# Value products of head pairs on the two halves of the output's rows, with the queries as columns, in block two's attentions

## What is computed

```
ya = spatial_gating(...)
yb = chunk_band_attention(heads(bq), heads(bk), heads(bv), b_rel)
yc = dsa_attention(heads(cq), heads(ck), heads(cv), iq, ik, iw, t5_table)
ym = memory_attention(heads(mq), km, vm)
mixed = concatenate([ya * silu(a_g), yb * silu(bg), yc * silu(cg), ym * silu(mg)])
y = mixed @ w_out + b_out
```

## Time and profile before

| | |
|---|---|
| Time, three runs | 3182.13 us median, 3174.91 to 3184.65 |
| The profiled execution: its own time and its span | 3182.28 us, span 3180.4 us |
| PE busy over the span | 3014.5 us (95%) |
| DVE, ACT, POOL busy | 1965.4, 1187.2, 490.2 us |
| The three attentions of block two | 1746 to 1948 us of the span |

### The profile page before, as it was taken

How to read it: one execution, slowest core, us unless ns; L and a number is a source line. 1 busy time by engine, 2 the same in 40 slices (tenths; PEclk the granted TensorE clock), 3 DMA queues, 4 the chain that set the end, 5 groups by cost and what they waited for, 6 DMA issues and landing times. The chain is left out here.

```text
span 3180.4 us, 38641 instructions
## 1 busy us (share of the span) xinstructions
PE 3014.5 (95%) x14576; PEld 2429.5 (76%) x14576; DVE 1965.4 (62%) x3282; ACT 1187.2 (37%) x2227; POOL 490.2 (15%) x465
## 2 busy tenths in 40 slices
PE   7999999999899999989999979999889999999999
PEld 6787876777788888777787878645668788888887
DVE  6111744699899946838988336799875444444444
ACT  2221331477677842224475554102561111111110
POOL 1000002355111100221244142010010000000000
PEclk9999999999899999999999989999899999999999
DMA  7323124543844334341255262311101111111111
GB/s 248 139 80 108 52 77 160 189 131 126 223 107 107 113 147 173 117 120 27 81 181 190 83 202 86 123 59 48 34 34 44 67 53 40 51 43 53 53 40 67
DMA packets 190771, 324.08 MB, mean 102 GB/s; under 512 B 16434, under 2 KB 113874, under 8 KB 190586
## 3 DMA queue, kind: packets, MB, share of 16 engines
q1 hardware_dynamic: 169722, 248.72, 25.4%
q0 software_dynamic: 20864, 72.89, 6.3%
HBM read 232.14 MB, written 88.11 MB: 101 GB/s over the span
## 5 line engine op out<-in xcount | busy, mean ns | idle before, releaser
L216 PE MATMUL banks<-b3mlpw_part,b3mlp_acthi 128*128 128x512 f32 x1024 | 315.4, 389 | 0.0
L216 PE MATMUL banks<-b3h4a_hi,b3mlpw_part 128*128 128x512 f32 x960 | 298.2, 389 | 2.1 <-DVE b3mlpw_part L3949 2.1
L428 PE MATMUL banks<-b1ln_w,b_hThi 128*128 128x512 f32 x768 | 239.8, 394 | 3.3 <-DVE b_hTlo L335 3.3
L3994 DVE TENSOR_TENSOR b3out_x<-b3out_x,banks 128x1024 f32<-128x1024 f32 x128 | 154.7, 1218 | 111.7 <-PE banks L216 111.7
L216 PEld LDWEIGHTS banks<-b3mlpw_part,b3mlp_acthi 128*128 128x128 f32 x1024 | 192.3, 188 | 39.9
L3965 ACT ACTIVATE b3mlp_relu<-banks 128x1024 f32<-128x1024 f32 x32 | 32.9, 1027 | 493.0 <-PE banks L216 493.0
L216 PEld LDWEIGHTS banks<-b3h4a_hi,b3mlpw_part 128*128 128x128 f32 x960 | 180.0, 188 | 43.2 <-DVE b3mlpw_part L3949 2.6
L530 PE MATMUL banks<-b_hThi,b1item_hi 128*128 128x512 f32 x464 | 196.4, 423 | 3.4 <-DVE b1item_lo L519 3.1
L216 PE MATMUL banks<-b3mlpw_part,b3mlp_actlo 128*128 128x512 f32 x512 | 199.4, 389 | 0.0
L216 PE MATMUL banks<-b3out_lo,b3mlpw_part 128*128 128x512 f32 x480 | 189.8, 395 | 0.0
L3983 DVE TENSOR_TENSOR b3mlp_relu<-b3mlp_relu 128x1024 f32<-128x1024 f32 x32 | 39.2, 1224 | 239.1 <-ACT b3mlp_relu L3965 239.1
(11 more groups left out here) (501 smaller groups left out, 6934.8 us busy)
## 6 DMA issues: line engine op xcount, KB each, us to landing
qk_spill<-b1scan_qk SPq DMA_DIRECT2D x64, 256.0 KB, 2.9
b1att_k<-qk_spill SPq DMA_DIRECT2D x64, 256.0 KB, 7.5
b1out_ws<-in_w_out SPq DMA_DIRECT2D x16, 1024.0 KB, 4.9
b3mlpw_stage<-in_w_mlp_down SPq DMA_DIRECT2D x16, 1024.0 KB, 4.9
b2h_stage<-in_w_in SPq DMA_DIRECT2D x30, 512.0 KB, 5.2
b3mlpw_stage<-in_w_mlp_up SPq DMA_DIRECT2D x15, 1024.0 KB, 5.1
b1item_stage<-in_w_in SPq DMA_DIRECT2D x29, 512.0 KB, 4.3
b1ln_stage<-in_w_in SPq DMA_DIRECT2D x12, 1024.0 KB, 5.2
```

The costliest lines, as they stand in the source:

```text
L216: last = pe.matmul(out, x, y, start=i == 0, stop=i == n - 1)
L428: last = pe.matmul(K.bank[n % 6], a, b, start=part + k + c == 0, stop=part + k + c == 6)
L3994: v.tensor_tensor(K.m4.x3[:, st], K.m4.x3[:, st], pair, ALU.add).then_inc(S["ml_acc"], 1)
```

## The change

The value products change sides. Before, `turned` (keys x queries) was the stationary operand and the values (keys x 64) the moving one, so that the queries were rows. Now a head's values (64 columns) are stationary and `turned` (128 queries) moves: the output is 64 rows x 128 queries, and heads h and h+1 go to rows 0 to 63 and 64 to 127 of the same columns, their products taking turns. Both heads of a pair are done in one round, r = u+5 for even u. The output is already in the layout of the gate, so the multiplication into `C.rows` and the two transposes are gone. Instead TensorE spreads 1/sum over rows with four products of a broadcast column and the unit matrix. VectorE multiplies the gate with them (in place), then the value products with that. The results of band and memory overwrite their own gates, and the stores read them there; the sparse ones go to `C.outT` as before. SyncE now waits for the stores before it loads over the gates.

```diff
@@ attention_rest, saved, sp_attend
     pass_stored(K, sp, A.kind + "g")
+    if A.sel:
+        saved(K, sp, K.m_band)
     for i in range(2):
         L.start(sp, (A.kind, "g", i), A.gate[:, i], K.pass_dram[A.kind + "g"][i, 0])
+def saved(K, e, A):
+    for i in range(2):
+        e.wait_ge(*K.stores[("b2y", A.k0 + i)])
     attended(K, sp, K.m_mem)
+    saved(K, sp, K.m_mem)
@@ pe_attend
-        u = r - 4
-        if 0 <= u < ALL_UNITS:
+        u = r - 5
+        if 0 <= u < ALL_UNITS and u % 2 == 0:
...
-            pe.wait_ge(S["at_copied"], u + 1)
-            out = K.bank[4 + T % 2][:, h * HD:(h + 1) * HD]
-            products(pe, out, [(C.turned[u % 3][:, i], val) for i, val in enumerate(A.vals(h, t))]).then_inc(S["at_av"], 1)
-        u = r - 6
-        if u >= 0 and u % 4 == 3:
-            T = u // 4
-            pe.wait_ge(S["at_norm"], T + 1)
-            for i in range(2):
-                last = pe.transpose(K.bank[4 + T % 2][:, 256 + i * P:256 + (i + 1) * P], C.rows[T % 2][:, i * P:(i + 1) * P], K.eye)
-            last.then_inc(S["at_flip"], 1)
+            pe.wait_ge(S["at_copied"], u + 2)
+            out = K.bank[4 + T % 2][:, h // 2 * P:(h // 2 + 1) * P]
+            vals = [A.vals(h + g, t) for g in range(2)]
+            for i in range(len(vals[0])):
+                for g in range(2):
+                    last[g] = pe.matmul(out[g * HD:(g + 1) * HD], vals[g][i], C.turned[(u + g) % 3][:, i], start=i == 0, stop=i == len(vals[0]) - 1)
+            for g in range(2):
+                last[g].then_inc(S["at_av"], 1)
+            if h == 2:
+                pe.wait_ge(S["at_one"], T + 1)
+                for i in range(4):
+                    spread = pe.matmul(K.bank[4 + T % 2][i % 2 * HD:(i % 2 + 1) * HD, 256 + i // 2 * P:256 + (i // 2 + 1) * P],
+                                       row_ones(K, T)[:, i:i + 1].to_broadcast([P, HD]), K.eye, start=True, stop=True)
+                    if i >= 2:
+                        spread.then_inc(S["at_flip"], 1)
@@ act_attend
-                a.wait_ge(S["at_av"], u - 2)
+                a.wait_ge(S["at_av"], (u - 3) // 2 * 2 + 2)
@@ dve_attend
-        u = r - 5
-        if 0 <= u < ALL_UNITS and u % 4 == 3:
...
-            v.tensor_tensor(C.rows[T % 2]..., K.bank[4 + T % 2][:, 0:256]..., over(row_ones(K, T), 2, HD), ALU.mult).then_inc(S["at_norm"], 1)
-        u = r - 7
+        u = r - 6
         if u >= 0 and u % 4 == 3:
...
-                if A.u0:
-                    for i in range(2):
-                        v.wait_ge(*K.stores[("b2y", A.last_k0 + i)])
...
+            v.wait_ge(S["at_flip"], 2 * T + 2)
+            gate, bank = A.gate[:, :, cols], K.bank[4 + T % 2].rearrange("p (a s) -> p a s", s=P)
+            v.tensor_tensor(gate, gate, bank[:, 2:4], ALU.mult).then_inc(S["at_norm"], 1)
+            v.wait_ge(S["at_av"], u + 1)
+            v.wait_ge(S["at_norm"], T + 1)
+            v.tensor_tensor(A.out[:, :, cols], bank[:, 0:2], gate, ALU.mult).then_inc(S["at_gate"], 1)
@@ memory map
+    band.out, mem.out, dsa.out = band.gate, mem.gate, C.outT
```

More of the change, by code:

```diff
@@ L3004, in pe_attend @@
             transposed(pe, bank_span(K, bank, width), [C.maps[u % 4][:, i * P:(i + 1) * P] for i in range(width // P)], K.eye).then_inc(S["at_turned"], 1)
-        u = r - 4
-        if 0 <= u < ALL_UNITS:
+        u = r - 5
+        if 0 <= u < ALL_UNITS and u % 2 == 0:
             A, h, t = stage_of(K, u)
-            T = u // 4
+            T, last = u // 4, [None, None]
             if u % A_UNITS == 0:
@@ L3093, in dve_attend @@
                 v.tensor_tensor_reduce(e, bank, bias, -1.0, 3e38, ALU.add, ALU.min, s[:, 0:1]).then_inc(S["at_shift"], 1)
-        u = r - 5
-        if 0 <= u < ALL_UNITS and u % 4 == 3:
[L3096 to L3101, removed]
-        u = r - 7
+        u = r - 6
         if u >= 0 and u % 4 == 3:
             A, h, t = stage_of(K, u)
+            T, cols = u // 4, slice(t * P, (t + 1) * P)
             if t == 0:
@@ L3107, in dve_attend @@
                     v.wait_ge(*K.loads[(A.kind, "g", i)])
-                if A.u0:
-                    for i in range(2):
-                        v.wait_ge(*K.stores[("b2y", A.last_k0 + i)])
-            cols = slice(t * P, (t + 1) * P)
-            v.wait_ge(S["at_flip"], u // 4 + 1)
-            v.tensor_tensor(C.outT[:, :, cols], K.bank[4 + u // 4 % 2][:, 256:512].rearrange("p (a s) -> p a s", a=2), A.gate[:, :, cols], ALU.mult).then_inc(S["at_gate"], 1)
+            v.wait_ge(S["at_flip"], 2 * T + 2)
[4 more added lines that the diff above has]
+            v.tensor_tensor(A.out[:, :, cols], bank[:, 0:2], gate, ALU.mult).then_inc(S["at_gate"], 1)
         if r == ALL_UNITS:
@@ L3147, in pool_attend @@
             for i in range(2):
-                K.stores.start(g, ("b2y", A.k0 + i), K.yT2_dram[A.k0 + i], C.outT[:, i])
+                K.stores.start(g, ("b2y", A.k0 + i), K.yT2_dram[A.k0 + i], A.out[:, i])
 def attend_over(K, e):
@@ L4132, in block_two_memory, with stage @@
     m.bs, m.g, m.b = a.take("bs", [P, 2, P]), a.take("g", [P, GW]), a.take("b", [P, GW])
-    def stage(kind, order, k0, last):
+    def stage(kind, order, k0):
         A = Part()
-        A.kind, A.u0, A.k0, A.last_k0, A.sel = kind, order * A_UNITS, k0, last, {}
+        A.kind, A.u0, A.k0, A.sel = kind, order * A_UNITS, k0, {}
         return A
@@ L4141, in queries @@
         A.v, A.gate = a.take(A.kind + "v", [P, 2 if A.kind == "m" else ST, GW]), a.take(A.kind + "g", [P, 2, S_LEN])
-    band, mem, dsa = K.m_band, K.m_mem, K.m_dsa = stage("b", 0, 2, None), stage("m", 1, 6, 2), stage("d", 2, 4, 6)
+    band, mem, dsa = K.m_band, K.m_mem, K.m_dsa = stage("b", 0, 2), stage("m", 1, 6), stage("d", 2, 4)
     a = Space(nc, "b2band", K.slots0, TOP)
@@ L4156, in block_two_memory @@
     C.turned = a.several("turned", 3, [P, ST, P])
-    C.rows = Space(nc, "b2rows", mem0 + 34 * 1024, mem0 + 36 * 1024).several("y", 2, [P, GW])
     ring = [stage_at(n, part) for n, part in USES2[-RING2:]]
```

## The result

The change takes 3191.24 us (median of 19 runs, 3182.16 to 3198.78) against 3182.13: a ratio of 1.0027, 95% interval 1.0017 to 1.0036, slower by 5 to 11 us. The profiled execution took 3194.97 us.

The account below looks back on a forecast made before the run. The prediction took a two-round loop through ScalarE's copy, not TensorE's work, as the bound. Longer loops (+18) and removed store waits (-14) gave +4 us on 3182.28: 3186 us, range 3181 to 3191.

Parts of the forecast that it names:

- The bound: In the attentions a two-round loop of waits bounds, not TensorE's work, which is 4.64 of 5.22 us in the wide band.
- the loop: Two rounds: transposes, value products, next unit's scores, then 2.75 us until ScalarE's copy, behind maximum and exponential, frees the banks.
- The sum for memory, 2.47: Memory's loop: value products 0.47, scores 0.32, then 1.68 us to the next waiting value products; the trace also has 2.47.
- The value products and the loops: Both heads of a pair, n products each, load the odd-round loop; it grows by 0.03n + 0.18 us wide, + 0.09 narrow.
- The price of a pair: New value products of two heads, n each, with entering and leaving their form: 0.238n + 0.18 us wide, + 0.09 narrow.
- The spreading: Four products for 1/sum behind a pair, once per query block: 0.48 us, net +0.33 without the two transposes.
- the term of 18: Loop growth over wide blocks (8.3 us) and 16 narrow ones (10.3), together +18.6, with the tail +18 us.
- The stores: VectorE's 5.03 and 6.39 us of store waits at memory's and sparse's first gates go, with refilling: -14 us.
- 39 us: no wait, but a margin of only 6: 27 rounds after the band's end take 39 us; the sparse table's quarters land 33 to 36.5 us after it.
- VectorE and SyncE: Two VectorE multiplications per query block run under TensorE's pair, and SyncE's new waits delay nothing needed: cost 0.
- Rival B: TensorE's clock falls to 1.2 GHz in half of the 64 narrow rounds: +12 us, 3198 us; chance 0.22.
- My +4: Whole kernel: 18 - 14 us added to the profiled 3182.28 us, giving 3186 us.

Follow-up runs that it names:

- e3: The change with ScalarE's copy of unit r-3's transposes moved ahead of the exponential of unit r: 3147.07 us, ratio 0.9887.
- e2: The change with all three results in the one shared buffer, VectorE's store wait back and SyncE's two store waits gone: 3198.05 us, ratio 1.0052.
- e4: The kernel before with ScalarE's copy of unit r-3's transposes moved ahead of the exponential of unit r: 3165.94 us, ratio 0.9947.
- e1: The kernel before with only band's and memory's results written over their gates and SyncE waiting for the stores; old value products: 3172.72 us, ratio 0.9968.
- e10: The change with the scores of each odd unit in the band's wide blocks computed twice: 3183.50 us, ratio 1.0.
- e8: The changed kernel measured once more, nothing altered: 3189.24 us, ratio 1.0024.
- e5: The change with pairs taken apart, each head's products in its own round, and the spreading behind head 3: 3186.93 us, ratio 1.0008.

## Why the prediction was right

**The bound.** Right. It said: "So the bound is the loop, and not TensorE's work". e3 cuts the loop by one move on ScalarE and gains 44 us on the change (39.4 in the attentions); e2 shows TensorE's saved work worth less than nothing while the loop stands. The sum for memory, 2.47, was no evidence for it: its three pieces are cut from one stretch of rows and must add up to it. There e3 and e4 are the evidence (4.21 for 5.74 us, 3.79 for 5.11).

**The value products and the loops.** Right in place and in the size of a block: a wide block 11.3 forecast and 11.3 measured, memory "5.6 to 5.7" and 5.74, pairs in odd rounds only, TensorE's wait once per two rounds (in memory 0.83 to 0.93 us, forecast 1.1). The price of a pair holds once it is read as a whole: its products take 1.24 us, the transposes ahead of it 0.70 where they took 0.58, the scores behind it 0.75 where they took 0.70. That is 1.24 + 0.12 + 0.05 = 1.41, forecast 0.238 x 5 + 0.18 = 1.37, and two rounds are 5.43 (forecast 5.4). The spreading costs 0.54 for 0.48. The sum over the blocks was too large. Against e1, which has the same gates, the blocks up to T = 14 and from T = 20 on add up to 7.3 (band) + 4.4 (memory) + 3.1 (sparse, from the first maximum of T = 20 to the projection) = 14.8, of which 3.2 are the clock. That leaves 11.6 for the loops; with 0.65 (memory's difference) for each of the five blocks between, where e1 waits for the table, it is 14.8, an estimate. From before to e2, where both wait for the stores, it is 13.5, of which 1.6 are the clock: 11.9. So the term of 18 was 12 to 15 in fact. Most is missing in the last block, from whose first maximum to the projection e2 takes 1.1 us less than the kernel before, in the first, where nothing was lost, and in those behind the waits for the stores.

**The stores.** Right in mechanism, too large in size: -14 forecast, and the attentions have -10.1 from before to e1 and -10.3 from e2 to the change. Behind both stand other losses: e1 waits 3.9 us for the table, and the change has the clock's fall of 1.6 in the last block that e2 has not. With these set aside it is -12 to -14, an estimate. The estimate "39 us: no wait, but a margin of only 6" held: the table is first touched 1868.4 - 1832.15 = 36.2 us behind the band's end, not 39, with half of that margin.

**VectorE and SyncE.** Right: no wait for `yT_spill`, none behind `saved`, and the two multiplications cost nothing where they stand.

**The clock.** Rival B was priced as half of the narrow rounds (+12). It came in the band and the sparse attention instead, twice for 1.6 us, and in memory, where I looked for it, the clock stayed at 1.00. This term was missing in the sum.

**Luck.** My +4 was 18 - 14. The attentions have +3.2, and as differences of whole kernels it is made of 13.3 to 13.5 for the products, the clock's 3.2 or 1.6 among them, and -10.1 to -10.3 for the stores. Both terms were some 4 us too large and cancelled, so that the sum comes so near is luck in part.

**The page on the clock.** The Trainium skill, TensorE: Matmul & The Clock Gate, "A second HAM failure mode", tells of an oscillation of the clock from frequent short idle times. The fall in the band, which goes when e10 fills the waits, agrees with it; but there are two falls in all, and the price is 3.2 us and not half of the rounds.

**The chances.** That the time would be the same within 0.3% had 0.60, and the measured ratio of 1.0027 lies there; the forecast's own range, 3181 to 3191, ends just under the median.

**What stays open.** The medians differ by 9.1 and, in the second measurement (e8), 6.5 us; both pairs of profiles have 3.2 in the attentions. Median less attentions is 2980 and 2983 for the two runs of before, 2986 and 2984 for those of the change, and 2981 to 2985 for all experiments. So some 3 us, and the same in e10's gain, are not in the attentions. Single profiles can't place them: ahead of the attentions, in code that no edit touches, they take from 1742.8 to 1752.8 us, the two of before 1746.4 and 1745.9, the two of the change 1752.4 and 1748.2, and behind them block three's falls of the clock differ from one execution to the next. Whether the change has a part in that, no run tells.

## What to carry to other kernels

Before giving an engine cheaper work, find the loop that ends its waits: add up one period from the rows, with pieces of other rounds, since pieces of the same stretch always add up. If the sum fits while the engine idles 14%, the work is not the bound. Then look which instruction stands ahead of the releasing one in another engine's fixed order; moving the copy ahead of an exponential that it did not need was worth 17 us on the kernel before and 44 on the change, more than either part of the change. Work that must be added belongs in the round that waits: while the loop stood, that was worth 12 to 14 us here for nothing. And a forecast of two terms of opposite sign is tested by a run of each alone, not by its sum.

## What was not expected of the hardware

- The two halves of the output's rows really run at the same time: ten products in 1.24 us, five alone in 1.23 (e5). The rows of e5 even show spreading products of one half (from 1784.40) starting between value products of the other (1784.51), though all of them come later in the program (head 3 writes rows 64 to 127, the first spreading product rows 0 to 63). The Trainium skill, TensorEngine Tiling (Array Packing), "Key Properties", says that tiles operate independently; the trace agrees.
- More work made the kernel faster: 5.6 us of repeated scores (8 x 0.70) cost nothing, and the median came out 5.7 to 7.7 us lower than the change's, of which the trace shows 3.2: two stretches at the lower clock that were gone. For the one in the band the filled waits are the likely cause; for the one in the sparse attention they can't be shown to be.
